# Taking the pre-norm of a projection out of the edge before it: the residual is turned as it is, and each token's factor is applied to the results

## The reference, cut to what matters

```python
def rms_norm_2(x, g):
    xf = x.astype(jnp.float32)
    y = xf * lax.rsqrt(jnp.mean(xf * xf, axis=-1, keepdims=True) + EPS)
    return (y * g.astype(jnp.float32)).astype(x.dtype)

    hn = rms_norm_2(h, attn_norm_g[l])
    proj = jnp.einsum('bsd,de->bse', hn, w_in[l])
    xc, b_gate, c_gate, q, k, v = jnp.split(proj, split_points, axis=-1)
    y_conv = short_conv_group(xc, b_gate, c_gate, conv_w[l], conv_out_g[l])
    y_attn = diff_attention_group(q, k, v, q_norm_g[l], k_norm_g[l], ...)
    mix = jnp.concatenate([y_conv, y_attn], axis=-1)
    h = h + jnp.einsum('bse,ed->bsd', mix, w_out[l])

# short_conv_group: y = b_gate * causal_depthwise_conv(c_gate * xc, conv_w), then rms_norm_2
#   over groups of 64 channels, with EPS, times conv_out_g
# diff_attention_group: q and k go through rms_norm_2 over each head's 64 channels, with EPS
```

## Time and profile before

| | us |
|---|---|
| median of 3 runs | 1125.33 (1125.15 to 1128.15) |
| profiled execution | 1126.19 |
| its span, first to last instruction | 1124.3 |
| PE busy | 961.5 (86%) |
| weight loads (PEld) | 714.9 (64%) |
| DVE busy | 483.2 (43%) |
| ACT busy | 385.9 (34%) |

### The profile page before, as it was taken

One profiled execution on the slowest core, in us unless ns is written; L12 is line 12 of the kernel. 1 busy time (PEld: TensorE's weight loads), 2 busy tenths in 40 slices (PEclk: granted clock), 3 DMA queues, 4 the chain that ended last, 5 costly groups with the idle time before them and its releaser, 6 DMA issues.

```text
span 1124.3 us, 14805 instructions
## 1 busy us (share of the span) xinstructions
PE 961.5 (86%) x5967; PEld 714.9 (64%) x5967; DVE 483.2 (43%) x806; ACT 385.9 (34%) x697; POOL 1.9 (0%) x7
## 2 busy tenths in 40 slices
PE   7999999999999999999999899949485767665667
PEld 6899899789778889998788675414141414132232
DVE  5656656765557655666856753110101010201010
ACT  4655445663765544555545430000000000000000
POOL 0000000000000000000000000000000000000000
PEclk9999999999999999999999999979788888887789
DMA  9746455744124454556231889999999999999996
GB/s 352 281 155 220 176 197 162 231 150 164 61 76 169 150 211 162 190 184 215 102 134 36 339 328 349 421 428 427 427 428 427 428 429 428 429 428 428 428 420 255
DMA packets 63425, 309.95 MB, mean 276 GB/s; under 512 B 2704, under 2 KB 3728, under 8 KB 53136
## 3 DMA queue, kind: packets, MB, share of 16 engines
q1 hardware_dynamic: 62944, 307.68, 69.2%
q0 software_dynamic: 432, 1.57, 0.4%
HBM read 308.19 MB, written 1.05 MB: 275 GB/s over the span
## 4 chain that ended last, share of the span: by engine, by line
PE 66%; DMA 17%; DVE 9%; ACT 4%; issue 2%; SPq 1%; DVEq 0%; ACTq 0%
DMA ring<-in_w_exp_down 16%; PE ps L679 14%; PE ps L680 14%; PE ps L681 14%; PE ps L1125 6%; PE ps L1175 6%; PE ps L1110 5%; PE ps L1187 3%; DVE w_lo L1745 2%; PE ps L874 1%; DVE w_lo L1732 1%; ACT w_hi L1304 1%; DMA scale_row<-in_pool_scale 1%; DVE hT_lo L1726 1%; SPq L635 1%
## 5 line engine op out<-in xcount | busy, mean ns | idle before, releaser
L1732 DVE TENSOR_TENSOR w_lo<-ring,w_hi 128x1024 fp32r<-128x1024 f32 x158 | 190.5, 1222 | 80.3 <-ACT w_hi L1289 80.3
L1125 PE MATMUL ps<-ring,x 128*32 128x512 f32 x992 | 131.6, 688 | 70.3 <-DMA ring<-in_w_exp_up 60.5
L679 PE MATMUL ps<-hT_hi,w_hi 128*128 128x256 f32 x656 | 187.3, 286 | 3.8 <-DVE hT_lo L1726 2.1
L1289 ACT ACTIVATE w_hi<-ring 128x1024 fp32r<-128x1024 f32 x158 | 164.1, 1053 | 76.1 <-PE ps L681 75.9
L680 PE MATMUL ps<-hT_lo,w_hi 128*128 128x256 f32 x656 | 186.1, 284 | 0.0
L681 PE MATMUL ps<-hT_hi,w_lo 128*128 128x256 f32 x656 | 186.1, 284 | 0.0
L1125 PEld LDWEIGHTS ps<-ring,x 128*32 128x32 f32 x992 | 38.2, 124 | 157.8 <-issue 155.4
L679 PEld LDWEIGHTS ps<-hT_hi,w_hi 128*128 128x128 f32 x656 | 126.4, 193 | 5.5 <-DVE w_lo L1732 2.9
L680 PEld LDWEIGHTS ps<-hT_lo,w_hi 128*128 128x128 f32 x656 | 126.4, 193 | 0.5
L681 PEld LDWEIGHTS ps<-hT_hi,w_lo 128*128 128x128 f32 x656 | 126.3, 193 | 0.0
L1175 PE MATMUL ps<-ring,moe 128*32 128x512 f32 x512 | 70.8, 711 | 55.3 <-DMA ring<-in_w_exp_down 53.9
(11 more groups left out here) (286 smaller groups left out, 1189.0 us busy)
## 6 DMA issues: line engine op xcount, KB each, us to landing
ring<-in_w_exp_gate SPq DMA_DIRECT2D x31, 2048.0 KB, 19.3
ring<-in_w_exp_up SPq DMA_DIRECT2D x31, 2048.0 KB, 19.9
ring<-in_w_exp_down SPq DMA_DIRECT2D x31, 2048.0 KB, 18.2
ring<-in_w_up SPq DMA_DIRECT2D x16, 2048.0 KB, 8.0
ring<-in_w_down SPq DMA_DIRECT2D x16, 2048.0 KB, 7.7
ring<-in_w_in SPq DMA_DIRECT2D x6, 2048.0 KB, 8.3
ring<-in_w_kv SPq DMA_DIRECT2D x4, 2048.0 KB, 10.2
ring<-in_w_q SPq DMA_DIRECT2D x2, 2048.0 KB, 9.8
```

Of the source, the lines that this page charges most:

```text
L679: mm(out, a_hi, b_hi, start=start, stop=False, skip_group_check=True)
L1125: last = mm(wk(side)[q, :], xgT[:, k, q], w4[:, j, k % 2, :] if opening else w[j][:, k, :], start=(k == 0), stop=(k == KD - 1))
L1289: fn(parts(n if edge else None, f)[0].rearrange("p (k w) -> p k w", k=KD), src, ACT.Copy).then_inc(hi_ready, 1)
L1732: ve.tensor_tensor(lo, src, hi.bitcast(F32), ALU.subtract).then_inc(lo_ready, 1)
```

## The change

Edge 2 gets the order of edges 0 and 1: `x` is turned, the second half's post-norm comes between the pairs of the turn, and both pre-norms are computed after it. `h` is no longer written and PE's 11 zero products go. Then DVE squares rstd, makes `epsm` = EPS * (mean square + EPS), which is EPS / rstd^2, and four diagonals (rstd^2 and epsm of each half). PE turns them into rows of all partitions by four products with ones in front of step 6, ACT copies them (`rows`, 512 wide) at step 7. The factors are applied so:

- q and k: their own norm takes `epsm` in place of EPS, in two small operations instead of one.
- v: ACT's copy gets the scale rstd.
- xc, c_gate and b_gate enter as a product of three. `xc` is multiplied by rstd^2 for both gated factors inside the convolution, now by DVE (line 2036 of the new kernel) instead of ACT's copy; b_gate's factor falls out in the norm behind it, whose mean squares get `epsm` (now DVE, line 2040) instead of EPS (in ACT's copy).

The diff, cut to its core:

```diff
 # PE
-            keep_busy(7, 11)
-            turn_half(h, 0, h_ready, 3, 4)
+            turn_half(x, 0, x_ready, 7, 4)
             keep_busy(7, 3)
             token_half(ps[:, 0, :], 0, 3, N_IN, 4 * (N_IN - 1) + 1)
-            turn_half(h, 1, h_ready, 4, 6)
+            turn_half(x, 1, x_ready, 8, 6)
...
+                if p == 6:
+                    pe.wait_ge(diag_ready, 6)
+                    for c in range(4):
+                        last = mm(ps[:, 7, c * P:(c + 1) * P], ones, diag2[:, c, :], start=True, stop=True)
+                    last.then_inc(rows_done, 1)
+                if p == 8:
+                    pe.wait_ge(rows_ready, 2)
 # ACT, edge_to_next
-                if edge == 2:
-                    pre_rsqrt(edge, 0)
-                else:
-                    for j in (0, 1):
-                        take_pair(turn, 0, j, bank, gain)
+                for j in (0, 1):
+                    take_pair(turn, 0, j, bank, gain)
                 post_half(edge, chunks, 1, scale)
...
+                for j in (2, 3):
+                    take_pair(turn, 0, j, bank, gain)
+                post_rsqrt(edge, 1)
                 take_half(turn, 1, bank + 2, gain)
-                if edge < 2:
-                    pre_half(edge, 1)
-                    pre_rsqrt(edge, 0)
-                    pre_rsqrt(edge, 1)
+                pre_half(edge, 1)
+                pre_rsqrt(edge, 0)
+                pre_rsqrt(edge, 1)
 # ACT, steps
             def wide_rsqrt(f):
-                act.wait_ge(ms2_done, f + 1)
-                fn(part(wms, f), ps[:, 5, 0:T], ACT.Copy, bias=EPS).then_inc(ms2_ready, 1)
                 act.wait_ge(ms2_ready, f + 1)
+                if p == 7:
+                    act.wait_ge(rows_done, 2)
+                    fn(rows[:, :], ps[:, 7, :], ACT.Copy).then_inc(rows_ready, 1)
                 if p == GATED:
+                    act.wait_ge(r2_ready, 3)
-                        fn(v2[:, s, :], ps[:, 6 + s, :], ACT.Copy).then_inc(v2_ready, 1)
+                        fn(v2[:, s, :], ps[:, 6 + s, :], ACT.Copy, scale=rstd[:, s:s + 1]).then_inc(v2_ready, 1)
-                    if r == 0:
-                        act.wait_ge(quarters_used, 4 * N_IN + p)
-                        fn(xc[:, f, :], ps[:, 3 + (p - 1) % 2, 0:T], ACT.Copy).then_inc(xc_ready, 1)
-                    elif r == 2:
+                    if r == 2:
                         conv_squares(f)
 # DVE, behind edge_to_next(2, ...)
+            square_rstd()
+            order(ve.tensor_scalar(epsm[:, :], ms[:, :], EPS, None, ALU.mult))
+            for s in range(TT):
+                ve.tensor_scalar(diag2[:, s, :], ident, rstd2[:, s:s + 1], None, ALU.mult).then_inc(diag_ready, 1)
+                ve.tensor_scalar(diag2[:, 2 + s, :], ident, epsm[:, s:s + 1], None, ALU.mult).then_inc(diag_ready, 1)
 # DVE, steps (behind the split of the weights, in front of conv_input and of the unit's work)
+                if GATED < p <= OUT and (p - GATED) % 3 == 1:
+                    f = (p - GATED) // 3
+                    dve.wait_ge(rows_ready, 2)
+                    dve.wait_ge(quarters_used, 4 * N_IN + p)
+                    ve.tensor_tensor(xc[:, f, :], ps[:, 3 + (p - 1) % 2, 0:T], rows[:, 0:T], ALU.mult).then_inc(xc_ready, 1)
+                if GATED + 4 <= p <= OUT + 1 and (p - GATED) % 3 == 1:
+                    f = (p - GATED - 4) // 3
+                    dve.wait_ge(ms2_done, f + 1)
+                    ve.tensor_tensor(part(wms, f), ps[:, 5, 0:T], rows[:, T:2 * T], ALU.add).then_inc(ms2_ready, 1)
```

More of the change, by code:

```diff
@@ L203, in build @@
         rstd2s = sb("rstd2s", [P, 2])
-        rows = sb("rows", [P, T])
+        rows = sb("rows", [P, 2 * T])
+        epsm = sb("epsm", [P, 2])
         st2 = sb("st2", [P, 2, 8])
@@ L246, in build @@
         e2 = at("e2", [P, 2, 2, T], scratch + 16 * K + 64)
+        diag2 = at("diag2", [P, 4, P], scratch + 16 * K + 64)
         moe = at("moe", [P, 2304], kqv)
@@ L1093, in _ @@
             keep_busy(7, 3)
-            pe.wait_ge(h_ready, 6)
+            pe.wait_ge(h_ready, 4)
             def experts(it, i2, u, first=False, last_pair=False):
@@ L1343, in edge_to_next @@
                 pre_half(edge, 0)
-                if edge == 2:
-                    pre_rsqrt(edge, 0)
-                else:
-                    for j in (0, 1):
-                        take_pair(turn, 0, j, bank, gain)
-                post_half(edge, chunks, 1, scale)
[L1350 to L1353, removed]
-                    pre_half(edge, 1)
-                    pre_rsqrt(edge, 1)
[L1356 to L1359, removed]
+                for j in (0, 1):
+                    take_pair(turn, 0, j, bank, gain)
+                post_half(edge, chunks, 1, scale)
+                for j in (2, 3):
+                    take_pair(turn, 0, j, bank, gain)
+                post_rsqrt(edge, 1)
                 take_half(turn, 1, bank + 2, gain)
-                if edge < 2:
-                    pre_half(edge, 1)
-                    pre_rsqrt(edge, 0)
-                    pre_rsqrt(edge, 1)
+                pre_half(edge, 1)
+                pre_rsqrt(edge, 0)
+                pre_rsqrt(edge, 1)
             def mlp(layer):
@@ L1464, in _ @@
                     act.wait_ge(rows_done, 1)
-                    fn(rows[:, :], ps[:, 3, T:2 * T], ACT.Copy).then_inc(rows_ready, 1)
+                    fn(rows[:, 0:T], ps[:, 3, T:2 * T], ACT.Copy).then_inc(rows_ready, 1)
                 if t in (21, 22):
@@ L1800, in square_rstd @@
                 ve.tensor_scalar(rstd2s[:, :], rstd2[:, :], 1.0 / 32, None, ALU.mult).then_inc(r2_ready, 1)
-            def normed_half(s):
-                ve.tensor_scalar(h[:, s, :], x[:, s, :], rstd[:, s:s + 1], None, ALU.mult).then_inc(h_ready, 1)
             def edge_to_next(edge, chunks, n, turn, gain, scaled2, bank=0):
@@ L1812, in edge_to_next @@
                 split(n, 2, quarter(n, 2))
-                if edge == 2:
-                    pre_mean(edge, 0)
                 post_half(edge, chunks, 1, scaled2)
[L1816 to L1820, removed]
                 for j in (0, 1):
                     take_pair(turn, 0, j, bank, gain)
[L1823 to L1827, removed]
+                split(n, 3, quarter(n, 3))
+                post_mean(edge, 1)
                 for j in (2, 3):
                     take_pair(turn, 0, j, bank, gain)
[L1830 to L1835, removed]
+                post_add(edge, 1)
                 take_half(turn, 1, bank + 2, gain)
-                if edge < 2:
-                    pre_half(edge, 0)
-                    pre_half(edge, 1)
+                pre_half(edge, 0)
+                pre_half(edge, 1)
             def mlp(layer):
@@ L1917, in _ @@
                 if 8 <= t < 16:
-                    ve.tensor_tensor(kT[:, t - 8, :], ps[:, f, 0:T], rows[:, :], ALU.mult).then_inc(proj_taken, 1)
+                    ve.tensor_tensor(kT[:, t - 8, :], ps[:, f, 0:T], rows[:, 0:T], ALU.mult).then_inc(proj_taken, 1)
                 elif t >= 16:
-                    ve.scalar_tensor_tensor(qT[:, t - 16, :], wk(f)[:, 0:T], DH ** -0.5, rows[:, :], ALU.mult, ALU.mult)\
+                    ve.scalar_tensor_tensor(qT[:, t - 16, :], wk(f)[:, 0:T], DH ** -0.5, rows[:, 0:T], ALU.mult, ALU.mult)\
                       .then_inc(proj_taken, 1)
@@ L1971, in head_sums @@
                 if s == 1:
-                    ve.tensor_scalar(qkst[:, 1, :], qkst[:, 0, :], 1.0 / 64, EPS, ALU.mult, ALU.add).then_inc(qk_mean, 1)
+                    for h2 in range(TT):
+                        c = slice(8 * h2, 8 * h2 + 8)
+                        last = ve.tensor_scalar(qkst[:, 1, c], qkst[:, 0, c], 1.0 / 64, epsm[:, h2:h2 + 1], ALU.mult, ALU.add)
+                    last.then_inc(qk_mean, 1)
             def head_scales(i):
```

## The result

The median of four runs is 1135.49 us (1133.86 to 1136.65), against 1125.52 (1125.15 to 1128.15) for the kernel before in the same comparison: ratio 1.0081, 95% interval 1.0064 to 1.0099. The medians differ by 10.0 us, and the interval of the ratio allows 7.2 to 11.1. The profiled execution has a span of 1134.1 us, 9.8 more than before.

A forecast was written before the change was run, and what follows sets the result against it. The expert stage's weight stream was taken as the bound, started by an SP issue that earlier delays push back. Terms 1.0 + 1.5 + 0.8 + 5.1 = 8.4 us gave 1134.6 profiled, 1133.7 as median; range 1128.6 to 1137.5.

The forecast's parts named there:

- Step 4 is held by the chain behind the lambda sums, not by PE: After the projection's second half: DVE's pre-norms, new operations and lambda sums delay the next split, 1.0 us later despite PE's gain.
- rival 5: At the changed edge: PE's early start survives, the split being ready sooner; -2.4 us, 1122.9, chance 0.06.
- The clock behind the gap: After PE's 4.7 us idle at the edge: 3.0 us at half clock lose 1.5 us, bounds 0 and 3.0.
- Rival 2: At the edge: the idle gap leaves the clock alone, 1.5 us less, 1132.2, chance 0.17.
- The stage: Attention and convolution, up to the SP issue: copies moved from ACT to DVE add 5.1 us, bounds 0 and 8.7.
- step 13: Start of the attention stage: xc now comes behind DVE's split, PE waits 1.2 us, DVE's maximum comes 1.0 us later.
- 16 and 19: Later steps of the attention stage: two added DVE operations between split and the unit's work cost 0.9 us each.
- Step 25: End of the attention stage: no unit's work between split and Newton's step, so the added sum's chain costs 1.4 us.
- rival 4: In the attention stage: DVE's gaps swallow the moved operations, leaving 3.3 us in all, 1128.6, chance 0.13.
- Rival 3: In the attention stage: PE's new waits bring two more low-clock stretches, +3.0 us, 1136.7, chance 0.14.
- Passed on in full: From the SP weight-load issue at 649.21, awaiting the last `mixT_lo`: any earlier delay, 8.4 us in all, moves the end equally.
- three conditions for being wrong: Step 4 starting before 553; its distance to the SP issue growing under 4 us; or the issue moving without the end.

The follow-up runs named there:

- b_late: Changed kernel with the splits of the first weights put ahead of pre-norms, diagonals and lambda sums on ACT and DVE: 1129.79 us, ratio 1.0035.
- a_warm: Changed kernel with 18 more products of zeros in PE's idle gap behind the projection's second half: 1131.45 us, ratio 1.0046.
- h_gap: Changed kernel with the four products with ones moved forward into PE's idle gap: 1136.4 us in one run.
- c_moved: Kernel before, its edge unchanged, with only the four xc copies and four mean-square copies moved from ACT to DVE: 1131.86 us, ratio 1.0047.
- d_both: Changed kernel with xc and mean-square copies both back on ACT, their row factors left out (for measuring only): 1131.8 us, ratio 1.0049.
- best: Changed kernel, splits first, lambda sums later, xc copied by ACT and multiplied by GpSimd, epsm row added by PE: 1123.6 us, ratio 0.9975 to before.
- d_wms: Changed kernel with only the four mean-square copies back on ACT, their factor left out; xc stays on DVE: 1130.47 us in one run.
- d_xc: Changed kernel with only the four xc copies back on ACT, their factor left out; mean squares stay on DVE: 1136.77 us in one run.

## Why the prediction was right, step by step

- **Step 4 is held by the chain behind the lambda sums, not by PE** (+1.0 forecast). Measured +0.77. The smaller size is DVE's pace: the seven new operations took 1.26 us (549.11 to 550.37) where 1.6 had been taken, as the four diagonals follow each other in 0.20 us and not 0.24; the pre-norms were done as computed (549.11 against 549.02). b_late shows the cause: with the norm, the diagonals and the lambda sums behind the split, PE's early start survives. That was rival 5, and it failed for the reason that the forecast gives.
- **The clock behind the gap** (+1.5 forecast). The mechanism held, the term was mis-sized: 2.7 by a_warm. The forecast took the 3.0 us of low clock behind the 1.97 us gap of the earlier trace rows; behind 4.42 us the clock was already low when step 4 began, and it stayed so for longer, through at least the 5.3 us of the window 554.9:560.2, half of which is 2.65. By the rule of the Trainium skill (TensorE: Matmul & The Clock Gate, section on HAM oscillation) a burst behind an idle gap starts cold. Here the trace agrees with it (0.50 from the first product of step 4 on); the earlier trace rows differ, where the fall came after the restart, behind a gap of less than half the length. Rival 2, no fall at all, is out.
- **Four products with ones** (+0.8). Measured 0.81, and 0.71 by h_gap. ACT's copy behind them cost nothing.
- **The stage** (+5.1). Measured +4.4 in the profile, +4.9 in c_moved, and +4.8 between d_both and h_gap; neither of these two has a low clock while PE works in the stage. The mechanism held at every step. By the table under d_both, step 13 gave 1.2 (1.0 forecast), and 16 and 19 gave 0.8 and 0.7 (0.9 each). Step 25 gave 1.33 (1.4), which leaves 0.7 for step 22 (0.9). That is 4.8; the profile shows 4.4 because the kernel before lost 0.4 at its low clock, a term that the sum did not have. That the steps pass on what is put into DVE's row, and that rival 4 (the gaps swallow it) is false, c_moved shows by itself. Rival 3 did not come in the changed kernel: its stage has one low-clock stretch before (0.92 over 600:622) and one after (0.86 over 638:650), and the latter cost nothing, since h_gap without it takes as long (75.67 against 75.68). In c_moved one more stretch came and cost 0.5.
- **Passed on in full.** The issue moved by 8.82 against 8.4, and the end by 9.8. One us was in no term. Part of it shows at the next loads that wait for PE, SP's rows behind the issue (before, after; in d_both it is 668.66):

```profile
666.17 1.06 SPq L635 DMA_DIRECT2D ring<-in_w_exp_down  x2
```

```profile
675.62 1.06 SPq L637 DMA_DIRECT2D ring<-in_w_exp_down  x2
```

They start 17.0, 17.6 and 15.4 us behind the issue. PE's clock near it is low over a short stretch before (0.51 over 650.3:653.7), over a long one after (0.51 over 656:663), and not at all in d_both. Nine of the ten profiles fall into this order. With no low clock there (d_both, best) the rows come at 15.4 and the span ends 474.1 to 474.7 us behind the issue. With the short stretch (before, d_wms, d_xc) it is 16.9 to 17.0 and 474.8 to 475.4. With the long one (after, b_late, c_moved) it is 17.5 to 17.6 and 476.0 to 476.2. h_gap has the long one and another at 680 to 684, and 18.2 and 477.4. The tenth, a_warm, has the short stretch and 17.0 but ends late (478.8), by something further back in its expert stage. What makes the stretch long stays open: PE's idle before the last turn is 2.91 us in the changed kernel, but 2.95 in a_warm and 2.98 in d_xc, which have the short one. No experiment took the stretch away by itself, so that it costs the us is argued and not shown. The sum so far: 0.8 + 2.7 + 0.8 + 0.2 + 4.4 + 1.0 = 9.9, against 9.8.

The forecast's 1133.7 came within 1.8 us partly by luck, because errors of both signs cancelled: the clock's term 1.2 too small and the last us missing, against a stage 0.7 below its term (0.3 of the copies, 0.4 of the low clock in the profile before) and step 4 0.2 below its. None of the three conditions for being wrong came true.

## What to carry to other kernels

When work is moved off one engine's path, ask first what the next thing on that path waits for: here PE was freed by 3.2 us, and the split that it needs next stood behind the very norm that had been moved out of its way. Put operands of the bounding engine first in the others' programs, and put behind them what is needed only later. In a cycle of hand-offs, an engine at 70% may have no gap in the place that counts: here each operation of 0.42 us moved onto DVE cost 0.5 to 0.6 us. An idle third engine can do better even at three and a half times the duration: with GpSimd's products and one product of PE the stage took 72.1 us instead of 75.7. And before a length is compared between two profiles, look for low-clock stretches in both: one of 3.4 us in the kernel before was worth 0.4 us, a tenth of the effect.

## What the runs showed of the hardware

- The granted clock fell without a long idle: in the kernel before it read 0.50 over 609.5:612.5, and between step 4 and there no wait of PE was over 0.76 us. Such a stretch cost 0.4 to 0.5 us there (before, c_moved), and nothing at 639 to 643 in the changed kernel.
- A gap of 4.42 us in front of work bound by PE cost 2.7 us more than itself; the same gap filled with products of zeros cost nothing, and the granted clock stayed at 1.00. Of idle before step 4, 3.19 us were enough for the low clock too.
- A product of two 128x256 float32 tiles on GpSimd took 1.43 to 1.51 us, against 0.42 for DVE's from an accumulator. Beside it DVE's `w_lo` kept its 1.23 us (at 595.40, with GpSimd's product from 595.72 to 597.22).
